# One attention phase for both head groups, with scores by query rows only and probabilities turned on TensorE

## The chip, the cores and the metric

The kernel runs on one core of one Trainium2 chip. The metric is the device time of one execution in microseconds (us); lower is better. The engines are TensorE (PE; its weight loads are listed apart as PEld), VectorE (DVE), ScalarE (ACT), GpSimd (POOL) and SyncE (SP), which here only issues transfers. Each engine works through its own queue in order and waits on semaphores that the others raise.

## The reference

The model is a two-layer backbone over 1024 latent tokens and 256 context tokens of width 1024. Layer 0 mixes tokens by pooling and a Fourier transform, layer 1 by windowed attention beside an RWKV-7 scan; each layer ends in a gated MLP. The change touches only the attention of layer 1. There are 8 query heads and 2 key/value heads of 64 channels, so a group is one key/value head with 4 query heads. What is computed, cut to what matters:

```python
def _axial_rope(x, pos_row, pos_col):      # rotates pairs of channels by cos/sin of the grid position
    ...
def _sink_attend(q, ks, vs, masks, sink):
    scale = HEAD_DIM ** -0.5
    logits = []
    for kt, m in zip(ks, masks):
        s = jnp.einsum('bqhgd,bkhd->bhgqk', q, kt).astype(jnp.float32) * scale
        if m is not None:
            s = jnp.where(m, s, -jnp.inf)
        logits.append(s)
    logits.append(jnp.broadcast_to(sink.reshape(HK, G, 1, 1).astype(jnp.float32), (B, HK, G, Q, 1)))
    p = jax.nn.softmax(jnp.concatenate(logits, axis=-1), axis=-1)
    ...                                     # sum of p @ v over the window's and the context's keys

# in the mixer of layer 1 (rows: 1024 latent tokens, 256 context tokens)
q = _axial_rope(_rmsnorm(q.reshape(B, T, N_Q_HEADS, HEAD_DIM), q_norm), pos_row, pos_col)
k = _axial_rope(_rmsnorm(k.reshape(B, T, N_KV_HEADS, HEAD_DIM), k_norm), pos_row, pos_col)
k_c = _rmsnorm(k_c.reshape(B, C, N_KV_HEADS, HEAD_DIM), k_norm)
# per block of 128 queries: keys of blocks i-1, i, i+1 with |i-j| <= 128, and all context keys
att = _window_attention(q, k, v, k_c, v_c, sink)
```

## The kernel before

`build` runs six phases one after the other: start, pooling and Fourier mixer, first MLP, attention, RWKV, second MLP. Between two phases `phase_over` frees the semaphores and makes all engines meet at a barrier. Around attention this is a hard edge: the projection before it writes q, k and v to DRAM (`z_scratch`), and the RWKV phase after it begins with its own loads. The attention phase is a loop of two passes, `per(2, lambda g: attention_phase(K, g))`, one for each group, with a barrier after each pass.

A pass has two parts.

**Preparation.** SP issues eight loads: the key rows of the group twice (for the lower and the upper 64 partitions), the constants `aux`, two tiles of queries (two heads each), the rotary table `tab`, v and the sink. ACT squares keys and queries (`square`, L1717), PE sums the squares by 2-column matmuls (`sums_of`, L1585), ACT takes the root (L1723), DVE the reciprocal (L1776). `factors` (L1598) spreads the reciprocals over 128 partitions by TensorE, `norm` (L1786) multiplies them in, for keys and queries alike. The rotation takes a matmul by a permutation (L1614), a product with the cosines on POOL (`cos_part`, L1563), one with the sines on DVE (L1798) and a sum (L1801). A product in float32 precision is made from pieces: each operand is kept as a rounded high part and a low rest, written by ACT (L1711, L1733, L1736), DVE (L1806, L1813, L1816) and POOL (L1569, L1575). No score is formed before all six chunks of 512 columns are through.

**Blocks.** For each of the 8 blocks of 128 queries the scores are formed twice. `scores` (L1630 to L1636) forms them by rows, queries on the partitions and up to 640 keys along the row, four heads one after the other, so that DVE can take each row's maximum (`maxima`, L1823 to L1834). `keyed_scores` (L1646 to L1653) forms them a second time with the keys on the partitions, one key tile for four heads at once (128x512), adds the mask and, by a matmul with rows of -maximum, subtracts the maximum; ACT turns that into probabilities (L1757), which lie as the product with the values needs them. For that subtraction the maxima are turned by PE (L1692) and spread by DVE (`spread`, L1841). `values` (L1662) multiplies each probability tile (stationary, 128x128) with v and a column of ones, whose product is the softmax denominator. `scale_out` divides (L1849 to L1853), `turn_out` turns the result (L1671), ACT copies it out (L1745).

The order is written by hand, one loop over blocks on each engine. In step i PE alternates a head of `scores` for block i+1 with a key tile of `keyed_scores` for block i, and ends the step with `values` of block i-1. The first and the last block of a group have 4 key tiles (two of the window, two of the context), the other six have 5.

## Time and profile before

| quantity | value |
|---|---|
| median of 3 runs | 3446.09 us (3443.47 to 3452.34) |
| the profiled execution: time, span | 3446.2 us, 3444.4 us |
| PE busy over the span | 3211.0 us, 93% |
| DVE, ACT, POOL busy | 45%, 23%, 26% |
| mean granted clock of TensorE | 0.964 |
| attention, first pass | 1682.83 to 1839.66 us |
| attention, second pass | 1839.66 to 1996.74 us |

The span runs from the first to the last instruction. Busy time counts a matmul from its start to its modelled end, and matmuls overlap, so a mean of one is longer than the distance from one start to the next. The edges of the passes are the starts of POOL's first instruction after each barrier.

### The profile page before, as it was taken

Reading aid. Unit: us, or ns where it says so; the run is one execution under the profiler, and the core shown is the slowest. Engines: PE = TensorE matmul, PEld = TensorE weight load, DVE = VectorE, ACT = ScalarE, POOL = GpSimd, SP = SyncE. Lnnn points to the kernel's source line nnn. Section 1 sums busy time; section 2 is a strip of 40 time slices with the busy share of each in tenths; the row PEclk is TensorE's granted clock in tenths of the full one; section 3 lists DMA queues with packets and bytes.
Section 4 is the critical chain, followed back from the end, with each engine's and each line's share of the span. In section 5 each row is a group of like instructions: output and inputs, shape, how many; then the busy total and the mean of one; then the engine's idle time right before and its main releaser. Section 6 shows DMA issues by size and latency. Waiting matters only on the chain. (4 is left out here: it accounts for less than half of the span.)

```text
span 3444.4 us, 65376 instructions
## 1 busy us (share of the span) xinstructions
PE 3211.0 (93%) x28356; PEld 2625.2 (76%) x28356; DVE 1538.5 (45%) x2389; ACT 784.9 (23%) x1486; POOL 887.6 (26%) x469
## 2 busy tenths in 40 slices
PE   5897999999999999999886979999987999999999
PEld 4653888888888888788675857777776788888887
DVE  4052444444444445512254446777655544433434
ACT  4001220000000001300222346666642311001100
POOL 3201323333333222433202000000004343343332
PEclk8999999999999999999897989999998999999999
DMA  5456001111111111122101020011012011111112
GB/s 223 152 186 220 31 29 39 37 37 37 42 39 38 37 40 40 62 83 77 70 1 53 0 65 25 28 31 35 23 34 90 25 61 45 48 49 49 49 43 74
DMA packets 67407, 202.09 MB, mean 59 GB/s; under 512 B 8017, under 2 KB 22609, under 8 KB 66898
## 3 DMA queue, kind: packets, MB, share of 16 engines
q1 hardware_dynamic: 63698, 183.73, 15.5%
q10 hardware_dynamic: 3456, 14.55, 1.0%
q8 instruction: 212, 3.47, 0.4%
q14 instruction: 41, 0.34, 0.0%
HBM read 177.41 MB, written 20.84 MB: 58 GB/s over the span
## 5 line engine op out<-in xcount | busy, mean ns | idle before, releaser
L155 POOL TENSOR_TENSOR w_hi<-w_raw,zero 128x1024 fp32r<-128x1024 f32 x158 | 304.1, 1925 | 1262.7 <-PE ps L167 804.4
L167 PE MATMUL ps<-u_hi,w_hi 128*128 128x512 f32 (+1 forms) x2232 | 602.2, 369 | 13.4 <-POOL w_lo L158 9.1
L167 PE MATMUL ps<-u_lo,w_hi 128*128 128x512 f32 (+1 forms) x2232 | 600.3, 369 | 0.0
L167 PE MATMUL ps<-u_hi,w_lo 128*128 128x512 f32 (+1 forms) x2232 | 599.8, 368 | 0.0
L787 DVE SCALAR_TENSOR_TENSOR ffn_cv<-ps,small,ffn_cv 128x1023 f32<-128x1023 f32 (+1 forms) x132 | 134.2, 1016 | 770.6 <-ACT ffn_cv L1138 769.0
L167 PEld LDWEIGHTS ps<-u_hi,w_hi 128*128 128x128 f32 x2232 | 387.2, 188 | 94.8 <-issue 15.2
L167 PEld LDWEIGHTS ps<-u_lo,w_hi 128*128 128x128 f32 x2232 | 387.4, 188 | 73.2
L167 PEld LDWEIGHTS ps<-u_hi,w_lo 128*128 128x128 f32 x2232 | 387.4, 188 | 73.1
L1138 ACT ACTIVATE ffn_cv<-ps,small 128x1280 f32<-128x1280 f32 (+1 forms) x88 | 107.8, 1225 | 1239.2 <-PE ps L167 1227.7
L158 POOL TENSOR_TENSOR w_lo<-w_raw,w_hi 128x1024 fp32r<-128x1024 f32 x158 | 383.3, 2426 | 12.4
L631 DVE SCALAR_TENSOR_TENSOR h<-ps,mod,h 128x1024 f32<-128x1024 f32 x210 | 206.6, 1013 | 139.0 <-PE ps L1087 138.6
L1087 PE MATMUL ps<-act_hi,w_hi 128*128 128x512 f32 (+1 forms) x800 | 225.4, 375 | 3.0 <-DVE h L631 2.6
L1087 PE MATMUL ps<-act_lo,w_hi 128*128 128x512 f32 (+1 forms) x800 | 221.5, 370 | 0.0
L1087 PE MATMUL ps<-act_hi,w_lo 128*128 128x512 f32 (+1 forms) x800 | 221.3, 370 | 0.0
L1087 PEld LDWEIGHTS ps<-act_hi,w_hi 128*128 128x128 f32 x800 | 138.7, 188 | 38.1 <-DVE h L631 13.6
L1087 PEld LDWEIGHTS ps<-act_lo,w_hi 128*128 128x128 f32 x800 | 141.0, 188 | 27.4
L1087 PEld LDWEIGHTS ps<-act_hi,w_lo 128*128 128x128 f32 x800 | 141.0, 188 | 26.9
L2293 POOL TENSOR_TENSOR rw_inv_k<-rw_ss_k,rw_expo 128x4 f32<-128x4 f32 x20 | 20.2, 1008 | 471.1 <-ACT rw_ss_k L2576 471.1
L789 DVE SCALAR_TENSOR_TENSOR ffn_cv<-ps,small,ffn_cv 128x1023 f32<-128x1023 f32 (+1 forms) x132 | 134.2, 1016 | 11.9 <-DVE ffn_cv L787 2.5
L2475 PE MATMUL ps<-rw_px,rw_x 64*64 64x64 f32 x3200 | 104.1, 229 | 3.6 <-DVE rw_px L2844 1.7
L787 DVE SCALAR_TENSOR_TENSOR cd_stage<-ps,small,cd_stage 128x1023 f32<-128x1023 f32 (+1 forms) x24 | 21.2, 883 | 181.2 <-ACT cd_stage L898 180.8
L2465 PE MATMUL ps<-eye,rw_xt 128*128 128x128 f32 x400 | 88.0, 302 | 11.7 <-ACT rw_az L2640 9.9
(374 smaller groups left out, 5009.5 us busy)
## 6 DMA issues: line engine op xcount, KB each, us to landing
w_raw<-in_ffn SPq DMA_DIRECT2D x132, 512.0 KB, 3.2
ada_ring_t<-in_ada SPq DMA_DIRECT2D x20, 512.0 KB, 5.6
w_raw<-in_cd_in SPq DMA_DIRECT2D x20, 512.0 KB, 3.9
z_scratch<-cd_stage ACTq DMA_DIRECT2D x15, 640.0 KB, 5.2
ada_ring<-in_ada SPq DMA_DIRECT2D x18, 512.0 KB, 5.9
ada_first<-in_ada SPq DMA_DIRECT2D x16, 512.0 KB, 15.6
ada_ring_s<-in_ada SPq DMA_DIRECT2D x14, 512.0 KB, 5.3
ada_ring_w<-in_ada SPq DMA_DIRECT2D x14, 512.0 KB, 6.3
```

What stands on the lines that cost most here:

```text
L155: pool.tensor_tensor(hi, K.raw[:, raw, :], K.zero[:, 0:1].to_broadcast([P, KT * P]), ALU.add).then_inc(self.hi_done, 1)
L158: pool.tensor_tensor(lo, K.raw[:, raw, :], hi, ALU.subtract).then_inc(self.split, 1)
L167: mm = pe.matmul(K.ps[:, slot, c, 0:width], wt[:, s, w], x[:, k, at:at + width], start=start and n == 0, stop=stop and n == 2)
L631: ins = dve.scalar_tensor_tensor(K.h[:, m, at:at + n], bank_cols(K, slot)[:, at:at + n], K.part(layer, part, m, c), K.h[:, m, at:at + n], ...
L787: chain.link(dve.scalar_tensor_tensor(cv[:, at + 1:at + n], psum[:, at:at + n - 1], w0, cv[:, at + 1:at + n], ALU.mult, ALU.add))
L789: last = dve.scalar_tensor_tensor(cv[:, at:at + n - 1], psum[:, at + 1:at + n], w2, cv[:, at:at + n - 1], ALU.mult, ALU.add)
L1087: mm = pe.matmul(o, wt, x[:, par, f, at:at + width], start=f == 0 and n == 0, stop=f == 1 and n == 2)
L1138: act.activation(cv[:, x, 0:n_tok], bank_cols(K, q % 2, cols), ACT.Identity, scale=tap(1, g, q)).then_inc(centre, 1)
L2293: pool.tensor_tensor(R.inv[:, :], R.ss[:, :], R.expo[:, :], ALU.pow).then_inc(inv_done, 1)
L2465: mm = pe.transpose(B2[:, 256 + h * P:256 + (h + 1) * P], xt[:, s, 2 * h:2 * h + 2, :].rearrange("p d c -> p (d c)"), K.eye[:, :])
L2475: mm = pe.matmul(bank(s, d)[HALF[c], P + h * CL:P + (h + 1) * CL], X[HALF[d], s, h, c * CL:(c + 1) * CL], PX[HALF[d], s, 2 * c + h, :], st ...
```

## The change

The two passes become one block of code. `attention_phase(K)` prepares only what the first blocks of group 0 need, runs 16 blocks in one loop (`NBLK`), and does the rest of group 0's preparation and all of group 1's in steps inside that loop. Tables (`FACTORS`, `TURNS`, `HIGHS`, `LOWS`, `SQUARES` and others) name the block and one of three places in it (1: after the first head of scores, 2: after the third, 3: at the end) at which an engine does such a piece. A piece is one of seven chunks of columns for each group; `K0B` is the first chunk of keys of group 1, `Q01` the queries of tile 0, second half, and so on.

The scores are formed once, by rows. The queries are stationary and hold the high part of a head in one half of the partitions and the low rest in the other; the keys stand as high and low parts in both halves. The mask is added for its two edge tiles only. The maximum is taken on the raw scores, and each query's normalising factor goes into the scale of the exponential (`exponents`, ACT reads the scores in PSUM, 512 or 640 columns, and also returns the sums of the rows), so queries are no longer multiplied by spread factors. The weight `q_norm` goes into the rotation matrix and a copy of the cosines. PE turns each 128x128 tile of probabilities (`turn_p`, four heads to a bank), ACT copies tiles 0, 2, 4 of a block to SBUF and DVE tiles 1 and 3 (`p_copy`); `values` uses them as stationary operand as before, with v's 64 columns. The denominator is the returned sum plus the sink's term, added on POOL (`sink_offset`, `denominators`). Each block's output is stored by a transfer of its own (16, before 4).

```diff
-def attention_phase(K, g):
+def attention_phase(K):
...
+    NBLK = 2 * NB
+    RING = 10
...
+    Pb = buf("p", [P, 2, 4, 5 * P])
+    pT = buf("p_turned", [P, RING, 4, P])
+    qs = buf("q_parts", [P, 4, SEQ], F32R)
+    khi = buf("k_hi", [P, 2, NT], F32R)
+    klo = buf("k_lo", [P, 2, NT], F32R)
...
+    CHUNKS = [(2, 0, 512), (2, SEQ, CTX), (0, 0, 512), (1, 0, 512), (2, 512, 512), (0, 512, 512), (1, 512, 512)]
...
+    K1, Q01, Q11, K0B, KCB, Q00B, Q10B, K1B, Q01B, Q11B = range(4, 14)
+    FACTORS = {(0, 1): K1, (4, 3): K0B, (5, 2): KCB, (8, 1): K1B}
+    TURNS = {(0, 3): K1, (1, 1): Q01, (1, 3): Q11, (5, 1): K0B, (5, 3): Q00B, (6, 1): Q10B,
+             (8, 3): K1B, (9, 1): Q01B, (9, 3): Q11B}
+    HIGHS = {(1, 1): K1, (1, 2): Q01, (2, 1): Q11, (5, 2): K0B, (5, 3): KCB, (6, 1): Q00B, (6, 2): Q10B,
+             (9, 1): K1B, (9, 2): Q01B, (10, 1): Q11B}
+    LOWS = {(1, 2): K1, (1, 3): Q01, (2, 2): Q11, (5, 3): K0B, (6, 1): KCB, (6, 2): Q00B, (6, 3): Q10B,
+            (9, 2): K1B, (9, 3): Q01B, (10, 2): Q11B}
+    SQUARES = {(2, 2): 2, (3, 1): 0, (3, 2): 1}
+    SUMS_K, SUMS_Q, ROOTS, INVERSES = (3, 2), (3, 3), (4, 1), (4, 2)
...
+            load_k(0)
...
+            sp.wait_ge(k_lo, 3)
+            load_k(1)
+            sp.wait_ge(q_lo, 4)
+            load_q(1, 0)
+            sp.wait_ge(q_lo_pool, 4)
+            load_q(1, 1)
...
+                w = qs[:, h, i * P:(i + 1) * P]
+                pe.matmul(o[:, 0:W], w, khi[:, g, ks[0] * P:ks[0] * P + W], start=True, stop=False)
+                pe.matmul(o[:, 0:W], w, klo[:, g, ks[0] * P:ks[0] * P + W], start=False, stop=False)
+                if len(ks) == 3:
+                    pe.matmul(o[:, 0:W].rearrange("p (t c) -> p t c", c=P)[:, 0::2, :], eye[:, :], band[:, 0::2, :],
+                              start=False, stop=True)
+                elif i == 0:
+                    pe.matmul(o[:, P:2 * P], eye[:, :], band[:, 2, :], start=False, stop=True)
+                else:
+                    pe.matmul(o[:, 0:P], eye[:, :], band[:, 0, :], start=False, stop=True)
+                for c, cw in ((0, P), (P, P)) if W + CTX > 512 else ((0, CTX),):
+                    pe.matmul(o[:, W + c:W + c + cw], w, khi[:, g, SEQ + c:SEQ + c + cw], start=True, stop=False)
+                    mm = pe.matmul(o[:, W + c:W + c + cw], w, klo[:, g, SEQ + c:SEQ + c + cw], start=False, stop=True)
+                mm.then_inc(scored, 1)
...
+            def turn_p(b, j):
+                if j >= len(tiles(b)):
+                    return
+                t = first[b] + j
+                if j == 0:
+                    pe.wait_ge(exp_done, 4 * b + 4)
+                if t < 2:
+                    pe.wait_ge(v_out, t + 1)
+                elif by_act[t - 2]:
+                    pe.wait_ge(p_act, act_upto(t - 2))
+                else:
+                    pe.wait_ge(p_dve, dve_upto(t - 2))
+                for h in range(4):
+                    mm = pe.transpose(pt_ps(t)[:, h * P:(h + 1) * P], Pb[:, b % 2, h, j * P:(j + 1) * P], K.eye[:, :])
+                mm.then_inc(p_turned, 1)
...
+            def values(b):
+                g = b // NB
+                if b >= 1:
+                    pe.wait_ge(y_done, b)
+                else:
+                    pe.wait_ge(v_out, 3)
+                pe.wait_ge(p_act, act_upto(first[b + 1] - 1))
+                pe.wait_ge(p_dve, dve_upto(first[b + 1] - 1))
+                ts = tiles(b)
                 for h in range(4):
                     for j, t in enumerate(ts):
-                        mm = pe.matmul(pv_ps[:, h, 0:65], pT[:, i % 2, j, h, :], vt[:, t, 0:65],
-                                       start=j == 0, stop=j == len(ts) - 1)
+                        mm = pe.matmul(y_ps[:, 64 * h:64 * h + 64], pT[:, (first[b] + j) % RING, h, :],
+                                       vt[:, t, 64 * g:64 * g + 64], start=j == 0, stop=j == len(ts) - 1)
...
+            for b in range(NBLK):
+                last = b + 1 == NBLK
+                turn_p(b, 0)
+                if not last:
+                    scores(b + 1, 0)
+                step(b, 1)
+                turn_p(b, 1)
+                if not last:
+                    scores(b + 1, 1)
+                turn_p(b, 2)
+                if b >= 2:
+                    turn_out(b - 2)
+                if not last:
+                    scores(b + 1, 2)
+                step(b, 2)
+                turn_p(b, 3)
+                if not last:
+                    scores(b + 1, 3)
+                turn_p(b, 4)
+                if b >= 1:
+                    values(b - 1)
+                step(b, 3)
+            turn_out(NBLK - 2)
...
+            def exponents(b, h):
+                g, i, s, n = b // NB, b % NB, b % 2, 4 * b + h
+                W = P * len(tiles(b))
+                act.wait_ge(topped, n + 1)
+                if h == 0 and b >= 2:
+                    act.wait_ge(p_turned, first[b - 1])
+                act.activation(Pb[:, s, h, 0:W], s_ps(n)[:, 0:W], ACT.Exp, bias=ntop[:, s, h:h + 1],
+                               scale=rms[:, g, 10 + 8 * (h // 2) + i, h % 2:h % 2 + 1],
+                               accum_out=tot[:, s, h:h + 1]).then_inc(exp_done, 1)
...
+                p_copy(b, 0)
+                if not last:
+                    exponents(b + 1, 0)
+                step(b, 1)
+                if not last:
+                    exponents(b + 1, 1)
+                p_copy(b, 2)
+                if not last:
+                    exponents(b + 1, 2)
+                if b >= 2:
+                    y_out(b - 2)
+                step(b, 2)
+                if not last:
+                    exponents(b + 1, 3)
+                p_copy(b, 4)
+                if not last:
+                    sink_exp(b + 1)
+                step(b, 3)
+            y_out(NBLK - 2)
+            y_out(NBLK - 1)
...
+                dve.reduce_max(mx[:, s, h:h + 1], s_ps(n)[:, 0:P * len(tiles(b))], AX.X).then_inc(maxed, 1)
+                dve.wait_ge(maxed, n + 1)
+                dve.scalar_tensor_tensor(ntop[:, s, h:h + 1], mx[:, s, h:h + 1],
+                                         nrq[:, g, 8 * (h // 2) + i, h % 2:h % 2 + 1], nsink[:, g, h:h + 1], ALU.mult,
+                                         ALU.min).then_inc(topped, 1)
...
+                    maximum(b + 1, 0)
+                step(b, 1)
+                if b >= 2:
+                    scale_out(b - 2)
+                invert_den(b)
+                p_copy(b, 1)
+                if not last:
+                    maximum(b + 1, 1)
+                if not last:
+                    maximum(b + 1, 2)
+                step(b, 2)
+                p_copy(b, 3)
+                if not last:
+                    maximum(b + 1, 3)
+                step(b, 3)
+            scale_out(NBLK - 2)
...
-    def per(n, phase):
-        def run():
-            with nc.Fori(0, n) as i:
-                phase(i)
-                K.phase_over()
-        return run
-
...
-              per(2, lambda g: attention_phase(K, g)),
+              lambda: attention_phase(K),
```

On PE, in a block in the middle of a group, one head of scores for the next block and one key tile of this block stood in this order before (att_q_hi, att_q_lo: parts of the queries; att_k_parts: of the keys; att_negT: rows of minus the maximum):

```order
L1630 MATMUL ps<-att_band,att_eye 128x384
L1631 MATMUL ps<-att_k_parts,att_q_hi 128x384
L1632 MATMUL ps<-att_k_parts,att_q_lo 128x384
L1634 MATMUL ps<-att_k_parts,att_q_hi 128x128
L1636 MATMUL ps<-att_k_parts,att_q_lo 128x128
L1634 MATMUL ps<-att_k_parts,att_q_hi 128x128
L1636 MATMUL ps<-att_k_parts,att_q_lo 128x128
L1646 MATMUL ps<-att_q_hi,att_k_parts 128x512
L1647 MATMUL ps<-att_q_lo,att_k_parts 128x512
L1649 MATMUL ps<-att_eye,att_band 128x512
L1653 MATMUL ps<-att_negT,att_one_8640 128x512
```

The same place now (L1763 turns a tile of probabilities, four heads; L1784 turns the output of an earlier block):

```order
L1763 MATMUL ps<-eye,att_p 128x128 x4
L1736 MATMUL ps<-att_k_hi,att_q_parts 128x384
L1737 MATMUL ps<-att_k_lo,att_q_parts 128x384
L1739 MATMUL ps<-att_band,att_eye 128x2x128
L1746 MATMUL ps<-att_k_hi,att_q_parts 128x128
L1747 MATMUL ps<-att_k_lo,att_q_parts 128x128
L1746 MATMUL ps<-att_k_hi,att_q_parts 128x128
L1747 MATMUL ps<-att_k_lo,att_q_parts 128x128
L1763 MATMUL ps<-eye,att_p 128x128 x4
L1784 MATMUL ps<-eye,att_y_scaled 128x128 x2
```

The three or four matmuls over 512 columns of a key tile are replaced by four transposes of 128 columns; the seven matmuls of a head stay, and the mask's is narrower.

On DVE the row of a middle block before:

```order
L1849 TENSOR_TENSOR att_den<-ps,att_sink_exp 128x4
L1850 RECIPROCAL att_rden<-att_den 128x4
L1853 TENSOR_TENSOR att_yn<-ps,att_rden 128x256
L1823 TENSOR_REDUCE att_max<-ps 128x1 x4
L1827 TENSOR_TENSOR att_top<-att_max,att_sink 128x4
L1831 TENSOR_TENSOR att_sink_off<-att_sink,att_top 128x4
L1832 TENSOR_SCALAR att_neg_hi<-att_top 128x4
L1833 CAST att_neg<-att_neg_hi 128x4
L1834 SCALAR_TENSOR_TENSOR att_neg<-att_top,att_neg_hi 128x4
L1841 TENSOR_TENSOR att_negT<-ps,att_aux 8x512
```

And now, from the maximum of the first head on (att_p_turned: a turned tile of probabilities copied out of PSUM):

```order
L2017 TENSOR_REDUCE att_max<-ps 128x1
L2019 SCALAR_TENSOR_TENSOR att_neg_top<-att_max,att_neg_rq,att_neg_sink 128x1
L2041 TENSOR_TENSOR att_y_scaled<-ps,att_rden 128x256
L2034 RECIPROCAL att_rden<-att_den 128x4
L2028 COPY att_p_turned<-ps 128x512
L2017 TENSOR_REDUCE att_max<-ps 128x1
L2019 SCALAR_TENSOR_TENSOR att_neg_top<-att_max,att_neg_rq,att_neg_sink 128x1
L2017 TENSOR_REDUCE att_max<-ps 128x1
L2019 SCALAR_TENSOR_TENSOR att_neg_top<-att_max,att_neg_rq,att_neg_sink 128x1
L2028 COPY att_p_turned<-ps 128x512
```

The four maxima no longer stand together: between the first and the second there are now the scaling of an earlier block, a reciprocal and a copy of 512 columns.

## Rows read from the trace of the kernel before

**Rows 1.** The page: busy us, share of the span, instructions by engine.
```profile
PE 3211.0 (93%) x28356; PEld 2625.2 (76%) x28356; DVE 1538.5 (45%) x2389; ACT 784.9 (23%) x1486; POOL 887.6 (26%) x469
```

**Rows 2.** Windows: us, busy PE, PEld, DVE, ACT, POOL; PEclk; DMA share; GB/s.
```profile
1682.83:1839.66 156.83, 125.30 (x790) 111.90 (x790) 68.14 (x136) 42.52 (x72) 20.22 (x13) 0.86 0.09 30
1839.66:1996.74 157.08, 125.09 (x790) 111.64 (x790) 68.15 (x136) 42.53 (x72) 20.14 (x13) 0.86 0.08 29
```

**Rows 3.** Windows by stage of the first pass.
```profile
1689.60:1708.20 18.60, 16.86 (x64) 14.21 (x65) 6.21 (x11) 3.95 (x5) 3.14 (x3) 0.50 0.30 105
...
1757.60:1770.20 12.60, 12.60 (x92) 11.82 (x91) 5.28 (x13) 3.46 (x7) 0.00 (x0) 1.00 0.01 2
...
1834.30:1839.70 5.40, 0.00 (x0) 0.00 (x0) 0.00 (x0) 0.00 (x0) 0.04 (x1) 0.56 0.49 194
```

**Rows 4.** Timeline of PE: start, us, line, count, idle before and its releaser.
```profile
1694.72 2.07 PE L1598 MATMUL ps<-eye,att_rms 128*128 128x128 f32 x8 [0.68 <-DVE att_rms L1776]
1696.59 3.41 PE L1585 MATMUL ps<-att_aux,att_sq 128*128 128x2 f32 x16
1701.71 1.91 PE L1614 MATMUL ps<-att_x,att_aux 128*128 128x512 f32 x2
1708.22 2.06 PE L1585 MATMUL ps<-att_aux,att_sq 128*128 128x2 f32 x16
1710.14 1.14 PE L1598 MATMUL ps<-eye,att_q_factor 128*128 128x128 f32 x8
1711.12 1.02 PE L1614 MATMUL ps<-att_x,att_aux 128*128 128x512 f32 x2
1732.26 0.55 PE L1630 MATMUL ps<-att_band,att_eye 128*128 128x256 f32 x1 [10.75 <-DVE att_k_parts L1816]
```

**Rows 5.** Timeline of PE in a middle block: turned output, a head, values.
```profile
1761.28 0.38 PE L1671 MATMUL ps<-eye,att_yn 128*128 128x128 f32 x2
1761.41 0.42 PE L1630 MATMUL ps<-att_band,att_eye 128*128 128x384 f32 x1
...
1763.40 0.34 PE L1630 MATMUL ps<-att_band,att_eye 128*128 128x384 f32 x1
...
1764.31 0.45 PE L1646 MATMUL ps<-att_q_hi,att_k_parts 128*128 128x512 f32 x1
...
1765.75 4.58 PE L1662 MATMUL ps<-att_vt,att_pT 128*128 128x65 f32 x40
```

**Rows 6.** Timeline of DVE: the end of a rotation beside POOL, and a maximum.
```profile
1721.93 1.73 DVE L1801 TENSOR_TENSOR att_x<-att_t 128x512 f32<-128x512 f32 x1
...
1744.59 0.83 DVE L1823 TENSOR_REDUCE att_max<-ps 128x1 f32<-128x640 f32 x1 [0.83 <-PE ps L1636]
1745.45 0.16 DVE L1827 TENSOR_TENSOR att_top<-att_max,att_sink 128x4 f32<-128x4 f32 x1
```

**Rows 7.** Groups by line and form, attention only: busy, mean ns; idle.
```profile
L1786 DVE SCALAR_TENSOR_TENSOR att_x<-att_x,small,ps 128x512 f32<-128x512 f32 x12 | 9.0, 748 | 18.1 <-PE ps L1598 18.1
L1798 DVE TENSOR_TENSOR att_t<-ps,att_tab 128x512 f32<-128x512 f32 x12 | 8.2, 685 | 4.1 <-PE ps L1614 4.1
L1853 DVE TENSOR_TENSOR att_yn<-ps,att_rden 128x256 f32<-128x256 f32 x16 | 6.8, 425 | 0.6
L1745 ACT COPY att_out<-ps 128x256 f32<-128x256 f32 x16 | 5.9, 368 | 19.5 <-PE ps L1671 19.5
```

**Rows 8.** Timeline of ACT: table load, an exponential, and a 640-column copy in RWKV.
```profile
1738.16 1.28 ACT L1751 ACT_TABLE_LOAD   x1 [12.36 <-DVE att_neg L1834]
1739.46 0.20 ACT L1751 ACTIVATE att_sink_exp<-att_sink_off 128x4 f32<-128x4 f32 x1
1740.12 0.60 ACT L1757 ACTIVATE att_pT<-ps 128x512 f32<-128x512 f32 x1 [0.46 <-PE ps L1653]
...
2016.16 0.70 ACT L2628 COPY rw_ts<-ps 128x640 f32<-128x640 f32 x1
```

**Rows 9.** Windows in the RWKV phase.
```profile
2100.00:2200.00 100.00, 95.46 (x2746) 76.61 (x2747) 66.24 (x169) 62.49 (x167) 5.00 (x5) 1.00 0.11 30
```

More of the change, by code:

```diff
@@ L1525, in attention_phase @@
-    yT_ps = K.ps[:, 1, 3, 2 * P:4 * P]
-    def keys(i):
-        return list(range(max(i - 1, 0), min(i + 1, NB - 1) + 1))
-    def tiles(i):
-        return keys(i) + [8, 9]
-    first = [sum(len(tiles(m)) for m in range(i)) for i in range(NB + 1)]
+    q_in, x_square = [S("q_in0"), S("q_in1")], S("square")
+    nrq_done = S("neg_rq")
+    consts, cosq_done, sums_done, root_done, inv_done = [S(x) for x in ("consts", "cos_q", "sums", "root", "inv")]
+    fac_done, normed, turned, cos_done, sin_done, roped = [
+        S(x) for x in ("factor", "normed", "turned", "cos", "sin", "roped")]
@@ new lines, in attention_phase, with keys, tiles @@
+    y_ps = K.ps[:, 0, 3, 0:256]
+    yT_ps = K.ps[:, 0, 3, 256:512]
+    def keys(b):
+        i = b % NB
+        return list(range(max(i - 1, 0), min(i + 1, NB - 1) + 1))
+    def tiles(b):
+        return keys(b) + [8, 9]
+    first = [sum(len(tiles(m)) for m in range(b)) for b in range(NBLK + 1)]
+    block_of = [b for b in range(NBLK) for _ in tiles(b)]
+    by_act = [j % 2 == 0 for b in range(NBLK) for j in range(len(tiles(b)))]
+    act_upto = lambda t: sum(by_act[0:t + 1])
+    dve_upto = lambda t: t + 1 - act_upto(t)
@@ new lines, in _ @@
+            pe.wait_ge(aux_in, 16)
+            sums_of(0, 2, bank(0), 0).then_inc(sums_done, 1)
+            factors(0)
+            factors(1)
+            sums_of(0, 0, bank(SPARE), 20)
+            turn(0)
+            pe.wait_ge(consts, 1)
+            turn(2)
+            sums_of(0, 1, bank(SPARE), 36).then_inc(sums_done, 1)
+            turn(3)
+            pe.wait_ge(v_in, 16)
+            for n in range(3):
+                turn_v(n)
+            pe.wait_ge(consts, 3)
+            for h in range(4):
+                scores(0, h)
@@ new lines, in _ @@
+            for b in range(NBLK):
+                last = b + 1 == NBLK
[19 more added lines that the diff above has]
+                step(b, 3)
@@ new lines, in _ @@
+            square(0, 2)
+            square(0, 0)
+            root(0, 0, bank(0))
+            square(0, 1)
+            high(0)
+            high(1)
+            root(0, 1, bank(SPARE))
+            for n in range(3):
+                v_copy(n)
+            high(2)
+            high(3)
+            for h in range(4):
+                exponents(0, h)
+            sink_exp(0)
+            for b in range(NBLK):
+                last = b + 1 == NBLK
+                p_copy(b, 0)
[16 more added lines that the diff above has]
+                step(b, 3)
@@ L1857, in _ @@
[L1857 to L1866 removed]
+            dve.tensor_copy(band[:, :, :].rearrange("p t c -> p (t c)"), band_in).then_inc(consts, 1)
+            invert(0, 0)
+            dve.wait_ge(tab_in, 16)
+            norm(0)
```

670 lines of the change are left out of this document (347 added, 323 removed).

## The prediction

> **What bounds the kernel now.** I read the page first: TensorE is busy for 93% of the span [rows 1], so what shortens the run is TensorE's work or its idle stretches. Windows over the two passes then give the size of what the change can touch: 156.8 + 157.1 = 313.9 us [rows 2]. The stages before and after lie behind barriers and keep their code. Third, the timeline of TensorE splits a pass. From the pass's start at 1682.83 to the first score at 1732.26 is 49.4 us of preparation; the last 10.75 us of it TensorE idles behind DVE, and from its first matmul on, 1689.6 to 1708.2, the granted clock is 0.50, the 1.2 GHz level [rows 3, 4]. A middle block lasts 12.5 us (1757.6 to 1770.2), with TensorE busy throughout at clock 1.00: the blocks are bound by TensorE. At the end 5.4 us pass with all engines idle, from the last store's issue to the barrier [rows 3]. So the two things on the path are TensorE's work in the blocks and, twice, preparation and exit.
>
> The sum is made against the profiled execution (3446.2 us; its span is 1.8 shorter, and nothing outside it changes); the median of the runs, 3446.09, is the same within 0.1.
>
> **Blocks: TensorE's work.** Before, a middle block's 12.5 us are 3.7 for four heads of scores (0.91 each, 1763.40 to 1764.31), 0.13 for turning the output (two transposes, 1761.28 to 1761.41), 4.4 for the values (40 instructions, 4.58 less the tail of the last one) [rows 5], and the rest, 4.3, for the key-major scores and the turned maxima. Now:
> - Scores: the mask's matmul shrinks from 384 to 256 columns; the 0.91 a head fall by some 0.07. 0.84 x 4 = 3.4 us.
> - Key-major scores go. Twenty transposes come. The row shows two of the same kind (float32, 128x128) in 0.13 us, 0.065 each: 20 x 0.065 = 1.3 us.
> - Values stay at 4.4 us: 64 columns instead of 65, but their distance of 0.11 us is more than 65 columns take at 2.4 GHz (0.027), so it does not hang on the columns.
> That is 9.2 us, 3.3 less than before.
>
> **Blocks: the chain.** These 9.2 us can't be had, because a head now goes PE, DVE, ACT and back before its PSUM banks are free for the head after next, and the engines' own orders put other work between. A block's step from its start, with 0.04 us for a hand-over (a maximum starts 0.04 behind the modelled end of its matmul) and 0.17 for a matmul's tail:
> turn 0.26, head 0 until 1.10, complete at 1.27; its maximum over 640 columns 0.83, then 0.03 and a small DVE operation of 0.16 [rows 6] until 2.32. Behind it in DVE's queue stand the scaling of an old block 0.42 [rows 7], a reciprocal 0.18 and the copy of a turned tile, which I take as the 0.685 of a 512-column product read from PSUM [rows 7]: until 3.6. Only then comes the maximum of head 1, which TensorE had finished at 2.4; its small operation ends at 4.6. ACT's exponential over 640 columns: 0.70, as the 640-column copy [rows 8], until 5.4. Head 3 needs the banks of head 1, so TensorE, idle since about 4.2, forms it from 5.4 to 6.3 and turns tile 4 until 6.5. The values share a bank with the turned output and wait for ACT to copy that out (0.37 [rows 7]), which stands behind the copy of tile 2 and the exponential of head 2: 6.9. Values 4.4: 11.3 us.
> Not shown before is the sum of a row that the exponential returns. Its cost lies between nothing and a small ACT operation of its own, 0.20 [rows 8]; two lie in the chain. I take half, 0.1 each, hardly mattering: 11.4 us to keep the table simple, against 12.5. TensorE is then idle about 2 of 11.4 us.
>
> **The sixteen steps.** Where the next block has 4 tiles, the chain is about 0.7 shorter, and values of 4 tiles take 3.55. Step 0 has no values to hide behind: 8.6 (one norm included). Steps 1, 8, 9 (4-tile values): 10.55 each; 2 to 5 and 10 to 13: 11.4 each; 6, 7, 14: 10.7 each; step 15: 6.9. Sum 8.6 + 31.65 + 91.2 + 32.1 + 6.9 = 170.5. The end: the last values 3.55 and, before and after them, 1.4 for scaling, turning and copying: 6.4. Together 176.9 us.
>
> **Preparation in the loop.** What it puts on the path depends on the place. At place 1 TensorE's piece (a rotation matmul 1.0, factors of 512 columns 1.1 [rows 4]) fits before the late maximum of head 1, but the two DVE operations of a rotation, 2 x 0.69, or a norm of 0.75 [rows 7], stand ahead of that maximum and are paid. At place 2 TensorE idles 1.2 us anyhow. At place 3 TensorE's piece is paid in full, and 0.4 of DVE's. That gives: rotations at place 1 (steps 1, 5, 6, 9) 4 x 1.4; at place 3 (1, 5, 8, 9) 4 x 0.9 and 4 x 0.4; key factors at step 4 1.0, norm at step 8 0.75. The sums of squares of group 1, 26 matmuls at 2.06 per 8 [rows 4]: keys 2.6 at place 2, of which 1.0 paid, queries 4.1 at place 3 paid. The two roots in step 4 need ACT's other table and the way back: 2 x 1.28 + 2 x 0.28 = 3.1 us, the load from [rows 8], with 1.6 of slack: 1.5. Sum 19.2 us. What hides the rest (squares, high parts, POOL's products and low parts) is ACT and POOL idle more than half of a step; their queues delay nothing that I can find, except that POOL must finish the low part of tile 1 of group 1 just as step 7 asks for it.
>
> **The first preparation.** Loads and clock stay as they are until the keys' factors (1694.7). Then: factors of 6 tiles 2.9, sums of one query tile 3.3, three rotations at 1.7 with another 3.3 of sums between them, as now at the low clock; the last rotation ends near 1709.5. DVE's pair on it until 1710.6; high parts on ACT behind the copies of the turned v until 1713.2; POOL's two low parts of 64x512 at half of a 64x1024 until 1715.5. First score at 1715.5, not 1732.26. The first four heads and ACT's table load go through the same chain at the low clock: 7.5 us, step 0 begins at 1723.0, 40.2 us after the start (before: 55.3).
> **Exit.** One, with a quarter of the bytes in the last store: 5.0 for 5.4.
>
> **Sum.** 40.2 + 176.9 + 19.2 + 5.0 = 241.3 against 313.9: 72.6 us less. 3446.2 - 72.6 = 3373.6; I give 3373. By origin: the second preparation, exit and first heads some 60, the first preparation 15, the blocks some 20, less 19 for the pieces in the loop (the parts overlap by a few us).
>
> **The skill weighed, twice.** The trace shows a table load of 1.28 us and the next activation starting 0.02 behind it [rows 8]. The Trainium skill, page "ScalarE: Activation LUTs", section "What ACT_TABLE_LOAD costs", adds a drain of 1.38 us to each switch; by it step 4 would be 2.8 us longer and the sum an estimated 3376.
> Two transposes start 0.065 us apart in the attention [rows 5]. The Trainium skill, page "TensorE: Matmul & The Clock Gate", section "Part 4: PE-mode transpose", gives about 275 ns for one in a kernel and says that such work does not count as busy for the clock. The trace has 0.27 only as one's length from start to modelled end, not as the distance. The clock part is rival D.
>
> **Rivals.**
> A. The forecast: 3373, own range 3355 to 3390.
> B. TensorE's work bounds the blocks after all, because the DVE copies and small operations overlap more than I add up. Each of some 14 full steps then costs 9.2: 14 x 2.2 = 31 less, 3342. For it: DVE's back-to-back operations show less distance than length. Against it: the wait for banks is in the code.
> C. Longer chain and collisions. If the steps cost as much as before (12.5; a sum of rows at 0.20, a copy at 0.8, TensorE-to-ACT hand-overs above 0.04), 14 x 1.1 = 15 more; an addition on DVE beside POOL took 1.73 instead of 0.69 [rows 6], with 10 such 10 more: 3398. For it: every hand-over now counts, where before TensorE had none to wait for.
> D. The slower side: TensorE's clock falls to its 1.2 GHz level in the blocks, since it idles 2 of 11.4 us and a part of its work is transposes. Values were 0.11 apart at the high level, and the 2-column matmuls of the sums, also bound by their weight loads, go from 0.13 to 0.21 each (2.06 and 3.41 for 16) [rows 4]; so values 8.5, scores 6.8, transposes 2.5: 18 us a step, 14 x 6.6 = 92 more: 3465. It decides from the point where the clock stays low for more than 11 of the 14 steps. Against it: in the RWKV phase TensorE runs at 1.00 with 64-column matmuls and transposes among them [rows 9]. The Trainium skill's sentence above speaks for it.
> E. The transposes are 0.27 apart: 14 x 2 (a part fills the idle time) = 28 more, 3401.
>
> **How the numbers follow.** A 0.60, B 0.10, C 0.20, D 0.05, E 0.05. A difference of 0.3%, 10 us, is about what a measurement of this kernel can tell from no change. A, B, C and E are all faster by more than that; 0.02 go to mixtures of C and a partly low clock that end within it. Faster 0.93, same 0.02, slower 0.05. The range holds A, most of C and E and the upper part of B: 3350 to 3402.
>
> **What would show it.** Right: a single attention stage of about 241 us; the first score some 33 us after its start; middle steps of 11.4 us (distance between the first transposes of blocks 11 and 12), with TensorE waiting for ACT's exponential before the fourth head and for the output copy before the values; clock 1.00 from step 1 on; a step 3 near 16.5. Wrong: middle steps of 9.2 to 9.6 (B) or over 12.3 (C), transposes 0.1 or more apart (E), a clock under 0.9 in steps 2 to 13 (D), or group 1's pieces adding more than 30 us.

## The result, and the profile after

The changed kernel took 3409.66 us (median of four runs, 3405.67 to 3411.11), the kernel before 3447.6 us; the ratio is 0.9888, 95% interval 0.9871 to 0.9905. It is faster by 38 us, not by the 73 us forecast, and lies outside the range. Its profiled execution took 3409.63 us with a span of 3407.8 us. The page, answering to [rows 1]:

```profile
PE 3191.4 (94%) x28314; PEld 2614.2 (77%) x28314; DVE 1528.4 (45%) x2364; ACT 813.2 (24%) x1585; POOL 879.5 (26%) x495
```

Now the windows of the attention stage: the whole of it (answering to [rows 2]), four stretches of steps 3, 7, 8 and 10, and two middle steps. Columns as in [rows 2]; the granted clock is the number behind POOL.

```profile
1684.94:1958.10 273.16, 230.49 (x1538) 211.60 (x1538) 125.87 (x247) 113.74 (x243) 33.02 (x53) 0.84 0.09 29
1765.00:1789.00 24.00, 24.00 (x114) 24.00 (x114) 3.46 (x8) 4.97 (x10) 0.40 (x2) 0.50 0.02 6
1835.90:1847.00 11.10, 11.10 (x55) 11.10 (x56) 0.99 (x3) 1.55 (x4) 0.40 (x2) 0.54 0.05 13
1853.00:1864.50 11.50, 11.15 (x46) 9.85 (x47) 2.60 (x5) 1.95 (x6) 2.84 (x4) 0.55 0.04 13
1884.50:1895.00 10.50, 10.50 (x51) 10.50 (x51) 0.52 (x2) 2.14 (x5) 0.40 (x2) 0.51 0.04 12
1900.64:1924.64 24.00, 22.35 (x182) 20.92 (x182) 11.62 (x24) 11.41 (x27) 0.80 (x4) 1.00 0.04 12
```

The stage takes 273.2 us against 313.9 in two passes before: 40.7 less, and 31.9 more than the 241.3 forecast. The whole execution gained only 36.6: the other 4.1 us came outside the stage, in code that did not change. The four stretches show a clock of .50 to .55, the 1.2 GHz level, with TensorE busy almost throughout: what it does there takes up to twice its time. The last row is two middle steps at 1.00: 12.0 us each.

TensorE's timeline shows what runs in those stretches (columns as in [rows 4]): the first score, then step 3 with the keys' sums, the values and the queries' sums.

```profile
1712.78 0.55 PE L1736 MATMUL ps<-att_k_hi,att_q_parts 128*128 128x256 f32 x1 [5.41 <-POOL att_q_parts L1644]
...
1763.33 2.64 PE L1688 MATMUL ps<-att_aux,att_sq 128*128 128x2 f32 x20
...
1769.19 8.63 PE L1777 MATMUL ps<-att_v_turned,att_p_turned 128*128 128x64 f32 x40
...
1777.62 6.93 PE L1688 MATMUL ps<-att_aux,att_sq 128*128 128x2 f32 x32
```

Forty instructions of the values take 8.63 us, where [rows 5] has 4.58. The first score comes 27.8 us after the stage's start, earlier than the 32.7 forecast.

A middle step at clock 1.00, timeline of all engines, only the chain: TensorE's first transposes, the maxima of heads 0 and 1, head 1's exponential and the reading of its row sum, the fourth head, the output's copy, the values, the next step.

```profile
1905.80 0.61 PE L1763 MATMUL ps<-eye,att_p 128*128 128x128 f32 x4
...
1907.30 0.82 DVE L2017 TENSOR_REDUCE att_max<-ps 128x1 f32<-128x640 f32 x1 [5.39 <-PE ps L1747]
...
1908.16 0.22 DVE L2019 SCALAR_TENSOR_TENSOR att_neg_top<-att_max,att_neg_rq,att_neg_sink 128x1 f32<-128x1 f32 x1
...
1908.92 0.69 DVE L2028 COPY att_p_turned<-ps 128x512 f32<-128x512 f32 x1
...
1909.53 0.81 DVE L2017 TENSOR_REDUCE att_max<-ps 128x1 f32<-128x640 f32 x1
...
1910.63 0.88 ACT L1901 ACTIVATE att_p<-ps,att_neg_top,att_rms 128x640 f32<-128x640 f32 x1 [1.24 <-DVE att_neg_top L2019]
1911.42 0.19 ACT L1901 ACTIVATION_READ_ACCUMULATOR att_p<-ps,att_neg_top,att_rms 128x1 f32 x1
...
1911.66 0.45 PE L1736 MATMUL ps<-att_k_hi,att_q_parts 128*128 128x384 f32 x1 [0.62 <-ACT att_p L1901]
...
1912.85 0.38 ACT L1922 COPY att_out<-ps 128x256 f32<-128x256 f32 x1
...
1913.28 4.68 PE L1777 MATMUL ps<-att_v_turned,att_p_turned 128*128 128x64 f32 x40
...
1917.79 0.61 PE L1763 MATMUL ps<-eye,att_p 128*128 128x128 f32 x4
```

The chain is the one the prediction walked, each link a little longer. Offsets from the step's start, forecast and measured: end of head 0's small operation 2.32, 2.58; maximum of head 1 starts 3.6, 3.73; its small operation ends 4.6, 4.80; exponential done 5.4, 5.81; values 6.9, 7.48; next step 11.3, 11.99.

ScalarE in step 4: the table loads for the two roots.

```profile
1789.25 1.28 ACT L1870 ACT_TABLE_LOAD   x1
1790.54 0.46 ACT L1870 ACTIVATE att_rms<-ps,epsc 128x20 f32<-128x20 f32 x2
1791.02 1.28 ACT L1901 ACT_TABLE_LOAD   x1
1792.31 0.88 ACT L1901 ACTIVATE att_p<-ps,att_neg_top,att_rms 128x640 f32<-128x640 f32 x1
```

The next activation stands 0.01 us behind each load; no drain comes on top.

A yardstick for what follows is the loop: from the first values of block 0 to those of block 14. The prediction's steps make it 168.2 us (from 8.4 us into step 1 to 2.5 us into step 15, added up), this execution 202.5 (1741.4 to 1943.9). It leaves out the preparation, which varied by itself (last section). The rest of the kernel varied too: what follows the stage's last output took 1448 to 1460 us in the profiles of this document. A run's profile is one of its executions, and a stretch seen in it need not be in the others.

### The profile page after: what moved, and what is told of

Same layout as the page of the kernel before. It is cut to its first block and busy times, and to the rows that moved or that the text cites. A ratio compares the mean times of both kernels' runs of the same rounds, so it can differ in the third digit from the quotient of the medians.

```text
span 3407.8 us, 65369 instructions
## 1 busy us (share of the span) xinstructions
PE 3191.4 (94%) x28314; PEld 2614.2 (77%) x28314; DVE 1528.4 (45%) x2364; ACT 813.2 (24%) x1585; POOL 879.5 (26%) x495
## 5 line engine op out<-in xcount | busy, mean ns | idle before, releaser
L789 DVE SCALAR_TENSOR_TENSOR ffn_cv<-ps,small,ffn_cv 128x1023 f32<-128x1023 f32 (+1 forms) x132 | 134.2, 1016 | 11.9 <-DVE ffn_cv L787 2.5
L2705 PEld LDWEIGHTS ps<-rw_px,rw_x 64*64 64x64 f32 x3200 | 80.1, 134 | 25.1 <-issue 15.9
```

What stands on the lines that cost most here:

```text
L789: last = dve.scalar_tensor_tensor(cv[:, at:at + n - 1], psum[:, at + 1:at + n], w2, cv[:, at:at + n - 1], ALU.mult, ALU.add)
L2705: mm = pe.matmul(bank(s, d)[HALF[c], P + h * CL:P + (h + 1) * CL], X[HALF[d], s, h, c * CL:(c + 1) * CL], PX[HALF[d], s, 2 * c + h, :], st ...
```

## The experiments

Each run's ratio is against the kernel before, timed beside it: 3448 us with the first four runs, 3451 and 3448 us later. The loop is read from the run's trace. Steps are counted by their block, and a distance "from values to values" belongs to the step in which it starts.

**The changed kernel again.**

> The changed kernel once more, as the base on this chip for the three that follow. The profile after shows four stretches at the granted clock .50 in the attention stage (steps 3, 7, 8 and 10: their times 26.2, 16.0, 17.9 and 17.15 us beside 11.4 to 12.8 for the steps at 1.00), 26 us more than those steps would have had. Theory A (few columns): they begin wherever TensorE passes from scores to the values (64 columns a matmul) or the sums of squares (2 columns), so each run shows three to five such stretches, and the time lies within 0.3% of 3410 us. Theory B (chance, or something outside this kernel): another run shows them at other places, in scores and transposes too, or none at all (about 3384 us).

3404.86 us, 0.9879 (0.9864 to 0.9895). The loop took 190.9 us. The windows of steps 7 and 10:

```profile
1833.80:1845.00 11.20, 11.18 (x57) 11.18 (x58) 1.36 (x4) 1.55 (x5) 0.40 (x2) 0.56 0.04 12
...
1882.40:1894.40 12.00, 11.17 (x91) 10.46 (x91) 5.80 (x13) 5.70 (x13) 0.40 (x2) 1.00 0.04 11
```

Steps 7 and 8 fell again, to the tenth of a us as before (17.5 and 18.2 from values to values); step 10 did not, and step 3's was short (19.6 us from values to values, not 25.8). The places recur, but not each one in each execution. Theory A holds in its places, with that looseness.

**Wide values.**

```diff
- mm = pe.matmul(y_ps[:, 64 * h:64 * h + 64], pT[:, (first[b] + j) % RING, h, :],
-                vt[:, t, 64 * g:64 * g + 64], start=j == 0, stop=j == len(ts) - 1)
+ vv = vt[:, t, 64 * g:64 * g + 64].rearrange("p (o c) -> p o c", o=1)
+ mm = pe.matmul(K.ps[:, 0, 3, 64 * h:64 * h + 128].rearrange("p (o c) -> p o c", o=2),
+                pT[:, (first[b] + j) % RING, h, :], vv.to_broadcast([P, 2, 64]), ...)
```

> Only the values' product is changed: its moving operand is the same 64 columns read twice, so each matmul has 128 columns and writes 64 columns that the next head overwrites. The result is the same. The values took 4.5 us for 40 instructions at clock 1.00 (114 ns each) and the wide ones should keep that pace if the weight load sets it (8.6 us if the columns set it: 16 steps x 4.1 us = 66 us slower). Theory A (the clock falls where a run of matmuls has few columns): the falls in steps 7, 8 and 10 vanish, 5.3 + 5.7 + 5.4 = 16.4 us, the one in step 3 stays since it begins in the sums: 3393 us. Theory C (idle gaps of TensorE just ahead, the waits for the exponentials, drop the clock whatever follows): no change, 3409 to 3411 us.

3391.94 us, 0.984 (0.9826 to 0.9854), against 0.9879 for the changed kernel. Windows of steps 7, 8 and 10:

```profile
1828.10:1840.80 12.70, 11.41 (x95) 11.03 (x95) 6.07 (x14) 5.11 (x12) 0.40 (x2) 1.00 0.03 10
1840.80:1854.30 13.50, 12.05 (x87) 10.29 (x87) 8.92 (x18) 5.81 (x14) 2.84 (x4) 1.00 0.04 12
...
1867.10:1879.20 12.10, 11.27 (x92) 10.55 (x91) 5.87 (x13) 5.70 (x13) 0.40 (x2) 1.00 0.04 11
```

The three falls are gone (12.7, 13.5, 12.1 us instead of 17.5, 18.2, 16.9), and a block's values keep 4.7 us with twice the columns. So the columns do not set their pace; the forty weight loads, the same in both, are what is left. Theory A's 3393 us came out at 3392. Theory C falls in its strict form: the same idle gaps stand ahead of the values, and the clock stays. It does not stay everywhere: step 3 falls in its sums as expected, and the wide values of step 4 took 6.36 us, with the clock at .50 for 3.4 of them.

**Wide sums.**

```diff
- mm = pe.matmul(o[:, cols + 2 * m:cols + 2 * m + 2], sq[...], hones[:, 0::64], ...)
+ mm = pe.matmul(o[:, cols + 2 * m:cols + 2 * m + P].rearrange("p (c h) -> p c h", h=2), sq[...],
+                hones.rearrange("p (h c) -> p c h", h=2), ...)   # group 1 only
```

> Only the second group's sums of squares are changed (step 3): the moving operand is the whole 128 columns in the order that puts the two wanted ones first, and the next matmul overwrites the 126 others. The result is the same. Theory A: the clock does not fall in the key sums of step 3; 52 instructions at 108 ns instead of 216 give 5.6 us, and the values there 4.5 instead of 8.6 us: 6 to 9.7 us less, 3400 to 3404 us, unless the values of step 3 start a fall of their own (then 4 to 6 us less). Theory C (idle gaps): no change.

3399.17 us, 0.9872 (0.9849 to 0.9895): not to be told from the changed kernel, with a wide spread (3392.36 to 3416.83; the profile is of the fastest). TensorE's timeline, the queries' sums of step 3 and the values of step 4:

```profile
1775.20 4.59 PE L1690 MATMUL ps<-att_aux,att_sq 128*128 128x128 f32 x32
...
1788.95 8.64 PE L1781 MATMUL ps<-att_v_turned,att_p_turned 128*128 128x64 f32 x40
```

The sums now run at full speed (4.59 us for 6.93), but the next narrow stretch, the values of step 4, took 8.64 us. A fall cured in one place came back 14 us later: the middle case of theory A.

The same profile shows something that none of the theories has. Its windows of steps 7, 8 and 10, where nothing was changed:

```profile
1834.80:1847.40 12.60, 11.33 (x94) 10.96 (x94) 6.01 (x14) 5.12 (x12) 0.40 (x2) 1.00 0.03 10
1847.40:1860.90 13.50, 12.02 (x86) 10.26 (x86) 8.91 (x18) 5.76 (x14) 2.84 (x4) 1.00 0.04 12
1873.80:1885.80 12.00, 11.18 (x91) 10.46 (x91) 5.83 (x13) 5.71 (x13) 0.40 (x2) 1.00 0.04 11
```

The values are as narrow as in the changed kernel, and the same waits stand ahead of them (0.80 and 0.66 us in step 7; 0.79 and 0.65 in the profile after), yet the clock stays at 1.00. So narrow values behind a gap do not bring the clock down each time.

**Both.**

> Both changes together. Theory A: no stretch at .50 after the first score; step 3 becomes 16 to 17 us and steps 7, 8 and 10 become 11 to 13 us: 26 us less, 3384 us. That would also say that of the 32 us which the attention stage took beyond the forecast, some 26 were the clock's and 6 the chain's. Theory C: no change, 3409 to 3411 us. Theory D (the longer chain per step carries the excess and the clock only fills idle time): at most 6 us less.

3386.78 us, 0.9824 (0.9811 to 0.9838); the loop takes 182.5 us, 20.0 less than in the profile after. TensorE's timeline, values and sums of step 3, values of step 4:

```profile
1766.18 4.63 PE L1782 MATMUL ps<-att_v_turned,att_p_turned 128*128 128x128 f32 x40
1770.65 4.54 PE L1690 MATMUL ps<-att_aux,att_sq 128*128 128x128 f32 x32
1784.39 6.09 PE L1782 MATMUL ps<-att_v_turned,att_p_turned 128*128 128x128 f32 x40
```

Two short falls are left, one that costs 1.5 us in step 4 and one of 1.7 in step 10, against the steps of the same kind at 1.00; both lie in wide values, with the clock at .50 for 3.4 us. So the clock cost the profile after 20.0 + 3.2 = 23.2 us of its loop; the expected time of 3384 was missed by 3.

**The order.** On top of both wide forms.

```diff
  # VectorE
-                invert_den(b)
-                p_copy(b, 1)
                 if not last:
                     maximum(b + 1, 1)
+                p_copy(b, 1)
...
+                invert_den(b)
                 step(b, 3)
  # ScalarE
+                if b >= 2:
+                    y_out(b - 2)
                 if not last:
                     exponents(b + 1, 2)
-                if b >= 2:
-                    y_out(b - 2)
```

> Built on the kernel with wide values and wide sums (3387 us), so that the clock disturbs little. VectorE scans the second scores ahead of its copy of the turned probabilities and inverts the denominators last; ScalarE copies the output block out ahead of the third exponential instead of behind it. In the middle steps (12.0 us from values to values) the fourth scores wait for the second exponential, whose maximum stands behind a reciprocal (0.18) and a copy (0.69). Theory A (the chain maximum, exponential, row sum sets the step where TensorE waits): the maximum ends 0.8 us earlier, the fourth scores start 0.7 to 0.8 us earlier, the step becomes 11.2 to 11.4 us, and 12 to 14 steps give 8 to 11 us: 3376 to 3379 us. Theory B (TensorE's own work bounds the step; waits move to other places): under 2 us.

3373.83 us, 0.9776 (0.9759 to 0.9794). Timeline of a middle step that begins at 1877.1, 10.9 us before its last row: maximum, exponential and row sum of head 1, the fourth head, the values, the next step.

```profile
1879.96 0.82 DVE L2023 TENSOR_REDUCE att_max<-ps 128x1 f32<-128x640 f32 x1
...
1881.07 0.89 ACT L1907 ACTIVATE att_p<-ps,att_neg_top,att_rms 128x640 f32<-128x640 f32 x1 [0.35 <-DVE att_neg_top L2025]
...
1881.86 0.19 ACT L1907 ACTIVATION_READ_ACCUMULATOR att_p<-ps,att_neg_top,att_rms 128x1 f32 x1
...
1882.12 0.42 PE L1740 MATMUL ps<-att_k_hi,att_q_parts 128*128 128x384 f32 x1
...
1883.53 4.63 PE L1782 MATMUL ps<-att_v_turned,att_p_turned 128*128 128x128 f32 x40
...
1887.99 0.60 PE L1767 MATMUL ps<-eye,att_p 128*128 128x128 f32 x4
```

The maximum of head 1 now starts 0.5 us behind the start of head 0's small operation (1879.49) and not 1.4 (1908.16 to 1909.53 in the profile after); the fourth head waits for nothing. The step is 10.9 us and TensorE is bound by its own work but for some 0.2 us. The gain, 13.0 us in the median and in the loop (169.5), is more than the 8 to 11 expected. Theory A. One fall is left in this profile, 6.8 us long, ahead of and in the values of step 4 (6.35 us).

**No row sums.**

> On the same base. It leaves out the row sums that the exponential accumulates (the denominators take constants instead). Theory A: the instruction that reads the accumulator (0.195 us) goes from the chain twice in a middle step, ahead of the third and of the fourth scores, and the exponential itself stays at 0.89 us for 640 columns: 12.0 becomes 11.6 to 11.8 us, 3 to 6 us over 16 steps: 3381 to 3384 us. If the accumulation also lengthened the exponential, it falls to about 0.70 us, the copy of 640 columns, and the step to 11.3 us: 3376 us. Theory B: no change.

3386.12 us, 0.9814 (0.9794 to 0.9834), against 0.9824 with them: no measurable difference. The denominators are constants here, and only the time is read. ScalarE's group of exponentials (count; busy us, mean ns):

```profile
L1908 ACT ACTIVATE att_p<-ps,att_neg_top,att_rms 128x640 f32<-128x640 f32 x48 | 42.7, 889 | 43.9 <-DVE att_neg_top L2025 43.8
```

It stays at 889 ns without the sum, so the 0.19 above the copy's 0.70 has another source (not tried: the scale and bias that it takes a partition at a time). The reading of the sum starts 0.1 us before the exponential's modelled end (1910.63 + 0.88 = 1911.51 against 1911.42 in the profile after), so only half of its 0.19 lengthens the chain, and a middle step goes from 12.0 to 11.9. Both expectations were too high; the prediction's 0.1 a sum was about right.

**No second preparation.**

> On the same base. It leaves out the whole preparation of the second group (loads, squares, sums, roots, factors, rotations, splits) and lets blocks 8 to 15 take the first group's keys and queries. The prediction priced what stands between the blocks for it at about 17 us of its 19.2 (the first group's second half stays). Theory A (the price is right): steps 3, 4, 5, 6, 8, 9 lose 15 to 20 us together: 3367 to 3372 us. Theory B (the pieces lie under the waits): under 8 us. Theory C (they cost more than priced, since the chain waits as well): 21 to 28 us, 3359 to 3366 us.

3367.06 us, 0.9751 (0.9731 to 0.9771), 20 us less than with it. The windows row of the stage, to the copy of the last output:

```profile
1683.80:1912.39 228.59, 192.72 (x1454) 176.78 (x1454) 110.46 (x222) 102.13 (x225) 19.78 (x42) 0.94 0.08 26
```

With it that stretch is 250.3 us. The loop is 160.7 us, 21.8 less than 182.5; 3.2 of them are the two short falls, which are gone here, so the pieces of the second group cost 18.6. The prediction has 16.5 for them (19.2 less 2.7 in step 1, which stay). Theory A. The profiled execution as a whole, the slowest of its four, gained only 10 us over that with the second preparation (3373.73 for 3383.77), since what follows the stage took 11 us longer in it; the price rests on the loop.

**Idle time filled.** On the changed kernel.

```diff
                 turn_p(b, 3)
+                if b in (7, 8, 10, 11, 12, 13, 14):
+                    ...                     # waits of blocks 7 and 10 for the bank
+                    for _ in range(3):
+                        pe.matmul(bank(SPARE), eye[:, :], khi[:, 0, 0:512], start=True, stop=True)
                 if not last:
                     scores(b + 1, 3)
```

> On the changed kernel itself, its values at 64 columns: three matmuls of 512 columns, whose result nobody reads, run in steps 7, 8 and 10 to 14 in the idle time ahead of the fourth scores (0.6 us, the three together 0.64 us at clock 1.00). Theory A (what counts is how many columns TensorE gets through, scores and values together): the falls in the values of steps 7, 8 and 10 vanish though the values are as narrow as before: 10 to 16 us less than the 3405 to 3410 us of the changed kernel. Theory B (the values' 64 columns alone bring it down, whatever ran ahead): the falls stay, 3405 to 3411 us.

3397.5 us, 0.9841 (0.982 to 0.9861), against 0.9879 (0.9864 to 0.9895) for the changed kernel. Windows of steps 7 and 8, with the values at 64 columns:

```profile
1831.20:1843.90 12.70, 12.06 (x97) 11.44 (x97) 6.12 (x14) 5.11 (x12) 0.40 (x2) 1.00 0.03 10
1843.90:1857.40 13.50, 12.02 (x87) 10.26 (x87) 8.91 (x18) 5.79 (x14) 2.83 (x4) 1.00 0.04 12
```

The falls are gone with narrow values as well (12.7 and 13.5 us again), and step 3, which got no fillers, still took 25.8 us. Up to step 7 this loop ran as in the profile after, to a tenth of a us from values to values, so the fillers are all that differs there. The narrow values alone do not bring the clock down: the gaps ahead of them have a part in it. Theory B falls.

**Order alone.** On the changed kernel, narrow values and sums.

> The new order alone, on the changed kernel with its 64-column values and 2-column sums (3405 to 3410 us). Theory A (order and clock are two separate losses that add): the middle steps at clock 1.00 become 10.9 us and the falls in the values stay: 10 to 13 us less, 3394 to 3398 us. Theory B (with TensorE's idle time gone ahead of the values the clock holds by itself, as with the fillers in those gaps): the falls in steps 7, 8 and 10 vanish too, step 3's stays: 20 to 28 us less, 3380 to 3388 us.

3382.74 us, 0.9808 (0.9792 to 0.9824). Windows of steps 7 and 8:

```profile
1836.30:1847.70 11.40, 11.16 (x97) 11.03 (x95) 6.61 (x14) 5.43 (x13) 0.40 (x2) 1.00 0.05 13
1847.70:1860.00 12.30, 11.69 (x88) 10.26 (x87) 8.60 (x18) 6.14 (x15) 2.85 (x4) 1.00 0.04 13
```

The order takes away most of the gaps, and with them the falls of steps 7, 8 and 10: 22 us less than the changed kernel's 3404.86, not 13. That is theory B's time. Its places are not quite theory B's: this profile, the slowest of the five, has no fall in step 3 but three others, of 13.7 us from the end of step 1 on, of 6.8 in step 4 and of 3.4 in step 7 ahead of the values. TensorE's timeline, the values of block 0, which take 3.7 us at 1.00:

```profile
1749.59 6.93 PE L1777 MATMUL ps<-att_v_turned,att_p_turned 128*128 128x64 f32 x32
```

The gains of the wide forms (18) and of the order (22) do not add: together they give 31.

**The first gap filled.** On the fastest version, twenty matmuls ahead of the first scores.

```diff
+            ...                             # waits for the operands
+            for _ in range(20):
+                pe.matmul(bank(4), eye[:, :], khi[:, 0, 0:512], start=True, stop=True)
             for h in range(4):
                 scores(0, h)
```

> Wide values, wide sums and the new order (3374 us), and on top twenty matmuls of 512 columns, read by nobody, in the 5.4 us that TensorE stands idle between the transposes of the values and the first scores. [...] Theory A (the idle gap brings the clock down): the first scores run at 1.00 and the steps begin 2 to 4 us earlier: 3370 to 3372 us. Theory B (VectorE and ScalarE set the first scores' pace): within 1 us. Theory C (twenty at clock .50 take 8.5 us and hold the first scores up by 3 us): 3377 us.

3375.73 us, 0.9792 (0.9773 to 0.9811), against 0.9776 (0.9759 to 0.9794) without: no gain that can be told. TensorE's timeline, the fillers and the first transposes of step 0:

```profile
1701.95 4.91 PE L1835 MATMUL ps<-att_k_hi,att_eye 128*128 128x512 f32 x20
...
1714.15 1.11 PE L1767 MATMUL ps<-eye,att_p 128*128 128x128 f32 x4 [1.94 <-ACT att_p L1911]
```

The first scores ran at 1.00, but the waits of 1.4 and 1.9 us for the first exponentials followed, and the step's first transposes run at half speed (1.11 us for 0.60). Without the fillers the granted clock was .50 for 13.7 us, from the gap into step 0; with them it fell later and for 6.8 us. The fall was put off and shortened, not removed. Closest to theory B.

The fastest version is thus the changed kernel with wide values, wide sums and the new order: 3373.83 us, 0.9776 of the kernel before, 31 us under the changed kernel.

## Why the prediction was wrong

**The step that failed is "clock 1.00 from step 1 on".** The fall to 1.2 GHz was there as rival D, but as all or nothing ("low for more than 11 of the 14 steps"), with 0.05; a partly low clock had a chance of 0.02 in a mixture and no price. What came is a fall in 4 of 16 steps. Its size had the right base: D's values of 8.5 us at the low clock were 8.6. Its argument against was weak: [rows 9] shows narrow matmuls at 1.00 where TensorE has hardly a gap (95.5 of 100 us busy). The forecast itself had made a step with 2 us of gaps and then 4.4 us of narrow matmuls, and [rows 9] has no such step.

Wide values, fillers and the new order each removed the falls of steps 7, 8 and 10 from their profiles by another road, and their ratios (0.9840, 0.9841, 0.9808 for 0.9879) say the same of their other executions. So narrow values and gaps both have a part in the falls. They are not the whole cause: with only the sums widened the same values behind the same gaps ran at 1.00, and with wide values step 10 still fell once, for 3.4 us. What decides it in an execution is open.

The Trainium skill, page "TensorE: Matmul & The Clock Gate", section "Part 4: PE-mode transpose", says that transposes don't count as busy in the same way; by it theirs would add to the gaps. No run here shows that apart: all keep the 304 transposes of the probabilities, those with the falls and those without.

**Where the 31.9 us are.** Preparation to step 0: 35.7 for 40.2, 4.5 less; the forecast kept the low clock, which here rose to 1.00 about 15 us after the start (in the repetition it rose after 29 and the preparation took 42.0). Step 0: 11.0 for 8.6, 2.4 more. The loop: 202.5 for 168.2, 34.3 more. Step 1 up to its values and the tail: 1.9 more. Exit 2.9 for 5.0: 2.1 less, and the sum is 32.0, with rounding. With the 4.1 us from outside the stage, which the prediction put at nothing, that makes the 36 us by which the profiled execution missed 3373.6. The loop's 34.3 are 23.2 of clock, 2.1 of pieces for the second group (18.6 for 16.5), and some 9 of longer steps: 0.6 to 0.7 in each of 14, as the run without the second group shows at clock 1.00 (12.0 for 11.4, 11.2 for 10.55 to 10.7).

**The middle step's 0.6 us.** Four terms were short. The exponential was sized by a copy of 640 columns, 0.70, plus 0.1 for the sum: it is 0.89, and with the sum 0.98. Four transposes and the way to the next matmul take 0.38 (1907.10 to 1907.48 in the profile after), 0.095 each and not 0.065, which was read from a pair. A head takes 0.94 (1907.48 to 1908.42), not 0.84: the smaller mask made it no shorter than the 0.91 of [rows 5]. Forty matmuls of the values take 4.5 (1913.28 to 1917.79), not 4.4. One reading was wrong without harm: the sums of squares are 52 matmuls at 2.06 us for 16 [rows 4], not 26 at 2.06 for 8, and the price of 6.7 us is the same. The DVE terms (0.83, 0.42, 0.18, 0.685 and the queue order) were met within 0.02, except the small operation, 0.22 for 0.16.

**Right.** The chain and its order, with TensorE waiting for the exponential ahead of the fourth head (0.62) and the values behind the output's copy; ordinary steps at a multiple of it; the price of the second group's pieces within 2.1 us; the first preparation some 15 us shorter (19.6 here, 35.7 for 55.3; 13.3 in the repetition). Rival B's 9.2 us were never there to be had: with the order repaired, TensorE's own work makes 10.9. Rival C's first half came partly true (steps of 12.0, between the forecast's 11.4 and its 12.5); of its collisions the profile shows one addition of 1.74 us beside POOL, in step 1. Rival E is wrong, though its mark of 0.1 is near. The drain of 1.38 us that the Trainium skill states (page "ScalarE: Activation LUTs", section "What ACT_TABLE_LOAD costs") is not in the trace.

The fastest version needs 169.5 us for the loop, 1.3 more than forecast. That its 3373.83 us are the number predicted for another kernel is chance: there the cost of heads and transposes was made up for by a better order.

## What to carry to other kernels

A change that takes work off TensorE can leave it with gaps and narrow matmuls, and the clock then takes a part of the gain back: give a falling clock a price for some of the steps, not only for all, and look for a gap followed by a run of narrow matmuls whose pace does not hang on their columns. There a wider moving operand cost nothing (128 columns took the 4.6 to 4.7 us of 64) and made the falls fewer and shorter. On the engine that feeds the chain, put what TensorE waits for ahead of copies and reciprocals: it paid twice, through the chain and through the clock. And where a fall comes and goes, read more than one execution, and each of its stretches, before a place is called cured.

## What the runs showed of the hardware

- In each fall of steps 7, 8 and 10 with narrow values the granted clock stayed at .50 for 10.2 us, though TensorE was busy almost throughout, scores included; those in wide values lasted 3.4 us, or 6.8 in the fastest version's step 4. One cured in step 3 returned in step 4.
- The row sum of an exponential is an instruction of its own, 0.19 us, of which 0.1 lies beside the exponential; its absence left that at 0.89 us for 640 columns.
- The stage's preparation took 37 or 43 us up to step 0's first copy in executions of the same code there (36.9 in the profile after, 43.2 in its repetition), so single executions differ by 6 us before the loop begins. It goes with the clock: the granted clock rose to 1.00 about 15 us after the start in the first and 29 us in the second. What sets the moment is not known.
- Still open: why the falls of steps 3, 7, 8 and 10 come in some executions only.
